# The beginning of a hybrid GLA/MLA/GQA trunk kernel: squares of the inputs first, two modulation blocks in a row, weight pieces and heads' weights later

## What is computed

```python
for l in range(DEPTH):                                   # DEPTH = 2
    shift, scale, gate = split(silu(c) @ w_mod[l] + b_mod[l], 3)          # latent tokens
    shift_c, scale_c, gate_c = split(silu(c_ctx) @ w_mod[l] + b_mod[l], 3)  # context tokens
    h  = rms_norm(x, norm_w[l]) * (1 + scale) + shift
    hc = rms_norm(ctx, norm_w[l]) * (1 + scale_c) + shift_c
    u, uc = split_cols(h @ w_in[l]), split_cols(hc @ w_in[l])
    y = concat(gla(u, uc), mla(u, uc), gqa(u, uc))       # three attention branches
    x = x + gate * (y @ w_out[l])                        # and ctx likewise in layer 0
return rms_norm(x, final_norm_w)
```

## Time and profile before

| | us |
|---|---|
| median of 3 runs | 1052.84 |
| lowest and highest | 1051.81, 1054.33 |
| the profiled execution | 1052.06 |
| its span in the profile | 1050.1 |
| TensorE busy in it | 963.9 (92%) |
| VectorE, ScalarE, GpSimd busy | 510.0, 421.4, 136.5 |
| mean granted TensorE clock | 0.971 of full |

### The profile page before, as it was taken

How to read it: one execution, slowest core, us unless ns; L and a number is a source line. 1 busy time by engine, 2 the same in 40 slices (tenths; PEclk the granted TensorE clock), 3 DMA queues, 4 the chain that set the end, 5 groups by cost and what they waited for, 6 DMA issues and landing times.

```text
span 1050.1 us, 12554 instructions
## 1 busy us (share of the span) xinstructions
PE 963.9 (92%) x4563; PEld 668.7 (64%) x4563; DVE 510.0 (49%) x872; ACT 421.4 (40%) x753; POOL 136.5 (13%) x158
## 2 busy tenths in 40 slices
PE   2789999999899999899899889899997999999896
PEld 2468889888465455455478677689774545445475
DVE  2535534532864444556452563543548444555443
ACT  4424433322113554656831432533321244555902
POOL 3000000001250001000640200000013300100720
PEclk9899999999889999999999899899999899999998
DMA  9802220311300232022053211130513000022022
GB/s 331 282 16 65 62 75 6 101 41 47 114 1 1 94 130 97 1 81 81 1 172 73 81 30 51 43 98 1 137 40 126 1 0 1 1 81 80 1 100 81
DMA packets 67867, 74.12 MB, mean 71 GB/s; under 512 B 6148, under 2 KB 47456, under 8 KB 67680
## 3 DMA queue, kind: packets, MB, share of 16 engines
q1 hardware_dynamic: 61392, 60.17, 18.2%
q0 software_dynamic: 4016, 12.77, 3.4%
q10 hardware_dynamic: 2400, 0.38, 0.2%
HBM read 69.11 MB, written 4.19 MB: 70 GB/s over the span
## 4 chain that ended last, share of the span: by engine, by line
PE 81%; DVE 7%; ACT 4%; issue 3%; DMA 2%; POOL 1%; ACTq 1%; DVEq 0%; POOLq 0%
PE pv L1692 10%; PE bank L1483 9%; PE bank L1484 9%; PE bank L1485 8%; PE bank L1743 6%; PE bank L1653 3%; PE bank L1774 3%; PE bank L1776 3%; PE bank L1775 3%; PE bank L1620 2%; PE bank L1600 2%; DMA W<-in_w_in 2%; PE bank L1669 2%; PE bank L1521 2%; PE bank L1523 2%
## 5 line engine op out<-in xcount | busy, mean ns | idle before, releaser
L1483 PE MATMUL bank<-hA_parts,W_parts 128*128 128x512 f32 (+1 forms) x496 | 181.7, 366 | 11.7 <-DVE h_low_parts L1016 9.1
L1484 PE MATMUL bank<-hA_parts,W_parts 128*128 128x512 f32 (+1 forms) x496 | 175.2, 353 | 0.0
L894 ACT ACTIVATE hA<-bank 128x512 f32<-128x512 f32 (+1 forms) x168 | 92.5, 561 | 82.1 <-PE bank L1743 56.1
L1290 DVE TENSOR_REDUCE mxp<-bank 128x1 f32<-128x384 f32 x192 | 96.4, 550 | 47.4 <-PE bank L1653 47.1
L1483 PEld LDWEIGHTS bank<-hA_parts,W_parts 128*128 128x128 f32 x496 | 95.7, 193 | 30.8 <-issue 14.0
L1485 PE MATMUL bank<-h_low_parts,W_parts 128*128 128x512 f32 (+1 forms) x310 | 109.9, 354 | 0.0
L1484 PEld LDWEIGHTS bank<-hA_parts,W_parts 128*128 128x128 f32 x496 | 95.6, 193 | 13.7 <-issue 2.2
L1692 PE MATMUL pv<-hA,vg 128*128 128x512 f32 (+1 forms) x168 | 83.1, 576 | 6.8 <-ACT hA L894 6.4
L1692 PE MATMUL pv<-hA,XA 128*128 128x512 f32 (+1 forms) x168 | 81.0, 563 | 2.4 <-ACT hA L894 2.3
L1023 DVE TENSOR_TENSOR W_parts<-W,W_parts 128x1024 fp32r<-128x1024 f32 x44 | 53.5, 1221 | 32.9 <-ACT W_parts L631 32.8
L1308 DVE SCALAR_TENSOR_TENSOR hA<-pv,hA 64x512 f32<-64x512 f32 (+1 forms) x36 | 21.6, 599 | 90.8 <-ACT hA L837 90.6
(11 more groups left out here) (254 smaller groups left out, 1836.6 us busy)
## 6 DMA issues: line engine op xcount, KB each, us to landing
W<-in_w_in SPq DMA_DIRECT2D x39, 512.0 KB, 4.0
W<-in_w_mod SPq DMA_DIRECT2D x8, 2048.0 KB, 8.0
W<-in_w_out SPq DMA_DIRECT2D x4, 2048.0 KB, 7.8
gqk<-in_w_mod SPq DMA_DIRECT2D x2, 1536.0 KB, 10.5
cqkv<-in_w_mod SPq DMA_DIRECT2D x2, 1536.0 KB, 14.7
XA<-in_x SPq DMA_DIRECT2D x4, 512.0 KB, 7.7
XA<-in_x POOLq DMA_DIRECT2D x4, 512.0 KB, 6.6
x_between_layers<-XA POOLq DMA_DIRECT2D x4, 512.0 KB, 2.9
```

The costliest lines, as they stand in the source:

```text
L894: act.activation(prob[slot % 4][:, 0:nq], ps("sc", l, h, q0, kt)[:, 0:nq], ACT.Exp, scale=MLA_SCALE if h < MLA_H else GQA_SCALE)\
L1290: dve.tensor_reduce(mxp[:, t, half:half + 1], ps("mx", l, h, q0, t, half)[:, 0:384], AX, ALU.max).then_inc(*up("part_max", l, h, q0, t, half))
L1483: pe.matmul(p[:, 0:c[1]], high[:, k, :], h_hi[:, k, toks], start=(k == 0), stop=False)
L1484: pe.matmul(p[:, 0:c[1]], low[:, k, :], h_hi[:, k, toks], start=False, stop=False)
```

## The change

ScalarE's queue starts with the identity. ScalarE no longer waits for the transposed vector tile before the squares: one table is loaded, the six tiles are squared, and only then the condition is computed, as exp(min(c,0) - ln(1 + exp(-|c|))) times c, with functions of that one table. TensorE transposes the vector tile behind the fourth input tile; VectorE copies it there and does its two steps of the condition between the copies of the last two tiles.

Modulation block 1 gets a ring bank and a row buffer of its own, so blocks 0 and 1 are multiplied in a row and then turned. ScalarE and VectorE take both blocks' rows and columns first, then units 0 and 1, slice 0, unit 2 and the other slices. TensorE multiplies block 2 after step k=0 and block 3 after k=1 of the product loop (before: after k=0 and k=2), and turns them after k=1 and k=2 (before: k=1 and k=3). GpSimd's `layer_weights(0)` moves behind the rearrangement of the narrow unit and a wait for block 3's products.

```diff
@@ -344,3 +344,7 @@
-            return pv_banks[0] if l == 0 and b < 4 else ps("mod", l, b)
+            return pv_banks[0] if l == 0 and b in (0, 2, 3) else ps("mod", l, b)
+        def modrow_of(l, b):
+            return cumA[:, 0:512] if (l, b) == (0, 1) else modrow
@@ -451,3 +455,2 @@
-            layer_weights(0)
             for l in range(DEPTH):
@@ -458,2 +461,5 @@
                 pool.memset(w_units[:, 0, 0, :, 32:64], 0.0).then_inc(*up("swap_kr", l))
+                if l == 0:
+                    pool.wait_ge(*at("filled", "mod", 0, 3))
+                    layer_weights(0)
                 pool.wait_ge(*at("wu_in", l))
@@ -551,2 +557,4 @@
         def _(act):
+            act.dma_start(con[:, C_ID:C_ID + P], a["consts"][:, C_ID:C_ID + P]).then_inc(*dma("ident_in"))
             def rows(r, n, src):
@@ -564,3 +572,2 @@
                     act.dma_start(vec[r:r + 2, half * 64:half * 64 + 64], a[name]).then_inc(*dma("vec_in"))
-            act.dma_start(con[:, C_ID:C_ID + P], a["consts"][:, C_ID:C_ID + P]).then_inc(*dma("ident_in"))
@@ -569,5 +576,2 @@
                 act.dma_start(w_units[:, 0, 0, :, o:o + n], src[:, :, c:c + n]).then_inc(*dma("w_small", 0))
-            act.wait_ge(*at("vec_turned"))
-            act.activation(ct[:, 0, :], vt[:, 0:16], ACT.Tanh, scale=0.5).then_inc(*up("cond_tanh"))
             act.preload_act_table_set("natural_log_exp_and_others")
@@ -578,5 +582,5 @@
-                    if (l, b) != (0, 0):
+                    if (l, b) not in ((0, 0), (0, 1)):
                         act.wait_ge(*at("filled", "modT", *((l, b - 1) if b else (l - 1, 3))))
-                    act.activation(modrow, mod_bank(l, b)[:], ACT.Copy).then_inc(*up("modrow", l, b))
+                    act.activation(modrow_of(l, b), mod_bank(l, b)[:], ACT.Copy).then_inc(*up("modrow", l, b))
                     let_go(("mod", l, b), "modrow", l, b)
@@ -655,2 +659,10 @@
                             turned_copy(t - 1)
+                    act.wait_ge(*at("vec_turned"))
+                    act.activation(ct[:, 0, :], vt[:, 0:16], ACT.Abs).then_inc(*up("cond_abs"))
+                    act.wait_ge(*at("cond_abs"))
+                    act.activation(ct[:, 0, :], ct[:, 0, :], ACT.Exp, scale=-1.0).then_inc(*up("cond_exp"))
+                    act.wait_ge(*at("cond_exp"))
+                    act.activation(ct[:, 0, :], ct[:, 0, :], ACT.Ln, bias=ones[:, 0:1]).then_inc(*up("cond_ln"))
+                    act.wait_ge(*at("cond_logsig"))
+                    act.activation(ct[:, 1, :], ct[:, 1, :], ACT.Exp).then_inc(*up("cond_sig"))
                     turned_copy(TILES - 1)
@@ -658,11 +670,13 @@
                     act.wait_ge(*at("xr_dve", TILES - 1, 1))
+                    mod_rows(0, 0)
+                    mod_rows(0, 1)
                     unit_high(0)
-                    for half in range(2):
-                        for b in range(2):
-                            mod_rows(0, 2 * half + b)
-                            if not half and b:
-                                unit_high(1)
-                                unit_high(2)
-                        for k in range(4):
-                            modulate(4 * half + k)
+                    unit_high(1)
+                    modulate(0)
+                    unit_high(2)
+                    for k in range(1, KD):
+                        if k == 4:
+                            mod_rows(0, 2)
+                            mod_rows(0, 3)
+                        modulate(k)
                     unit_high(3)
@@ -939,15 +953,19 @@
         def _(dve):
-            dve.wait_ge(*at("filled", "vec"))
-            dve.tensor_copy(vt[:], ps("vec")[:, 0:V_ROWS]).then_inc(*up("vec_turned"))
-            let_go(("vec",), "vec_turned")
-            dve.wait_ge(*at("vec_turned"))
-            dve.tensor_scalar(vth[:], vt[:], 0.5, None, ALU.mult).then_inc(*up("vec_half"))
-            dve.wait_ge(*at("cond_tanh"))
-            dve.wait_ge(*at("vec_half"))
-            dve.wait_ge(*at("pool_init", "end"))
-            dve.scalar_tensor_tensor(out=sc[:, :, 0:2].rearrange("p k s -> p s k"),
-                                     in0=ct[:, 0, :].rearrange("p (s k) -> p s k", s=2), scalar=1.0,
-                                     in1=vth[:, 0:16].rearrange("p (s k) -> p s k", s=2),
-                                     op0=ALU.add, op1=ALU.mult).then_inc(*up("cond_silu"))
+            def condition(part):
+                if part == 0:
+                    dve.wait_ge(*at("filled", "vec"))
+                    dve.tensor_copy(vt[:], ps("vec")[:, 0:V_ROWS]).then_inc(*up("vec_turned"))
+                    let_go(("vec",), "vec_turned")
+                if part == 1:
+                    dve.wait_ge(*at("cond_ln"))
+                    dve.scalar_tensor_tensor(out=ct[:, 1, :], in0=vt[:, 0:16], scalar=0.0, in1=ct[:, 0, :],
+                                             op0=ALU.min, op1=ALU.subtract).then_inc(*up("cond_logsig"))
+                    dve.wait_ge(*at("cond_sig"))
+                    dve.wait_ge(*at("pool_init", "end"))
+                    dve.tensor_tensor(sc[:, :, 0:2].rearrange("p k s -> p s k"),
+                                      vt[:, 0:16].rearrange("p (s k) -> p s k", s=2),
+                                      ct[:, 1, :].rearrange("p (s k) -> p s k", s=2), ALU.mult)\
+                        .then_inc(*up("cond_silu"))
+                    dve.tensor_scalar(vth[:], vt[:], 0.5, None, ALU.mult).then_inc(*up("vec_half"))
@@ -1007,2 +1025,5 @@
                     turned_copy(t - 1)
+                if t == TILES - 2:
+                    condition(0)
+            condition(1)
             turned_copy(TILES - 1)
@@ -1026,11 +1047,13 @@
                 if l == 0:
+                    mod_cols(0, 0)
+                    mod_cols(0, 1)
                     unit_low(0)
-                    for half in range(2):
-                        for b in range(2):
-                            mod_cols(0, 2 * half + b)
-                        if not half:
-                            unit_low(1)
-                            unit_low(2)
-                        for k in range(4):
-                            split_hidden(4 * half + k)
+                    unit_low(1)
+                    split_hidden(0)
+                    unit_low(2)
+                    for k in range(1, KD):
+                        if k == 4:
+                            mod_cols(0, 2)
+                            mod_cols(0, 3)
+                        split_hidden(k)
                     unit_low(3)
@@ -1422,7 +1445,2 @@
-            pe.wait_ge(*at("vec_in"))
-            pe.wait_ge(*at("ident_in"))
-            p = open_("vec")
-            close(pe.transpose(p[:, 0:V_ROWS], vec, ident[0:V_ROWS, 0:V_ROWS]), "vec")
             def mod(l, b):
@@ -1430,5 +1448,5 @@
                 if l == 0 and b < 4:
-                    p, w = mod_bank(l, b), early[b % 2]
-                    if b:
-                        pe.wait_ge(*at("modrow", l, b - 1))
+                    p, w = open_("mod", l, b) if b == 1 else mod_bank(l, b), early[b % 2]
+                    if b >= 2:
+                        pe.wait_ge(*at("modrow", l, b - 1 if b > 2 else 0))
                     pe.wait_ge(*at(f"w_early{b % 2}", b))
@@ -1458,3 +1476,3 @@
                     for f in range(4):
-                        mm = pe.transpose(q[:, P * f:P * f + P], modrow[:, P * f:P * f + P], ident)
+                        mm = pe.transpose(q[:, P * f:P * f + P], modrow_of(l, b)[:, P * f:P * f + P], ident)
                     close(mm, "modT", l, b)
@@ -1466,2 +1484,3 @@
+            pe.wait_ge(*at("ident_in"))
             for t in range(TILES):
@@ -1474,2 +1493,6 @@
                     close(mm, "xr", t, half)
+                if t == TILES - 3:
+                    pe.wait_ge(*at("vec_in"))
+                    p = open_("vec")
+                    close(pe.transpose(p[:, 0:V_ROWS], vec, ident[0:V_ROWS, 0:V_ROWS]), "vec")
@@ -1490,2 +1513,3 @@
                 mod(0, b)
+            for b in range(2):
                 mod_turn(0, b)
@@ -1497,6 +1521,9 @@
                         close(mm, "F", 0, item, c)
-                if k in (0, 2):
-                    mod(0, 2 + k // 2)
-                if k in (1, 3):
-                    mod_turn(0, 2 + k // 2)
+                if k == 0:
+                    mod(0, 2)
+                if k == 1:
+                    mod_turn(0, 2)
+                    mod(0, 3)
+                if k == 2:
+                    mod_turn(0, 3)
```

## The result

The changed kernel takes 1040.28 us in the median (1039.05 to 1041.91, 4 runs) beside 1052.32 for the kernel before (1050.71 to 1054.33, 4 runs): a ratio of 0.9885 with a 95% interval of 0.987 to 0.9901. 1041.6 had been forecast.

What follows compares the result with a forecast made beforehand. TensorE, 81% of the chain of waits, was taken to bound the kernel through early idles and half clock behind them. 9.5 + 1.7 = 11.2 us off 1052.06 gave 1040.9, median 1041.6; own range 1039 to 1044, overall 1036.5 to 1047.5.

Steps and rivals of the forecast that it cites:

- The sum: Whole run: 9.5 us at the product loop's fifth step plus 1.7 from the second half-clock stretch, 11.2 us gained.
- step 4: Heads' weights issued later: block 1's weights land near 25, the three pieces at 28.4 to 29.1; moved transfers cost nothing.
- Step 1: Squares first: first square at 9.94 instead of 15.86, 5.92 us earlier; three small condition steps add 0.75.
- Step 2: Modulation blocks 0 and 1 back to back, 1.9 us each; columns at 29.95, 6.4 us gained there.
- Step 3: Weight pieces behind the rows: first product of hidden values at 34.1 against 40.35, 6.25 us earlier.
- rival (a): Freed DMA time does not reach the other queues, landings stay: gain 8.1 us, 1044.7; chance 0.17.
- Step 5: Blocks 2 and 3 earlier in product loop: idle 0.65 instead of 3.70, fifth step 54.2 against 63.72, 9.5 us.
- The clock term: Second half-clock stretch, behind the fifth step's idle, goes with that idle: 1.7 us, half of its 3.40.
- Rival (c): Something else holds the fifth step at the second stall; only the start's 6.25 us remain: 1046.6; chance 0.07.
- (b): The first half-clock stretch at the first products shrinks too, giving back 1.9 us: 1039.7; chance 0.08.
- (d): Low clock persists over the first steps; if twice as long, 1.9 to 3.4 us lost: 1043.5 to 1045; chance 0.05.
- (e): TensorE's clock stays at half from first product through all eight steps: slower, 1065; chance 0.02.

Runs made afterwards that it cites:

- squares only: Kernel before with only the identity first, squares first and the condition behind them in one table's functions; 1052.56 us, ratio 0.9998.
- one-bank run: Changed kernel with blocks 0 and 1 sharing one bank and row buffer again, each turned before the next is multiplied; 1042.49 us, ratio 0.9902.

## Why the prediction was right

**The sum.** 11.2 was forecast up to the eighth step; the traces show 11.76 there, and the medians differ by 12.0 and, with the changed kernel once more, by 11.6. The forecast of 1041.6 is 1.3 above the measured median, inside its own range of 1039 to 1044.

That it came so close is in part luck. The first product came 1.4 us before the forecast, the fifth step only 0.7: the low stretch took half of it back. And two misses covered each other. With the start a microsecond early, block 1 began at 24.79 and the rounding of piece 1 near 28.2; step 4 had their weights land near 25 and at 28.4 to 29.1, which would have been late for both. They landed at 23.6 and 27.7.

**Step 1** had the right place; block 0 started 1.0 before the forecast. The three small steps behind the copies took 0.69 (0.75 was said), no table load appeared among them, and the vector transpose was hidden. What I missed is that ScalarE's own issues got shorter: its queue's last two transfers took 1.10 to issue, and the first square came at 9.05 rather than 9.94. Counting it in the sum would have given 1040.7. The same two took 1.08 with the identity first and the weights early (squares only: 1.06), 1.36 with the identity behind and the weights late, 2.17 with both as before. By these rows, of one execution each, either edit shortens them, and the identity's new place does so by itself.

**Step 2** held: from block 0's start it is 1.74 us to block 1's (1.9 was said) and 5.8 to the columns at 28.85 (5.9 was said). The second bank is worth the 1.4 us at the first product that the one-bank run shows.

**Step 3** held in the main: from the columns to the first product 3.9 us, and 4.15 was said. Its claim that the pieces belong behind the rows is not borne out for piece 0: the run with it ahead shows 0.8 us less idle, and with one bank the new order brought nothing at the first product. For pieces 1 and 2 no run puts them ahead. The start's gain comes from the squares, the late weights and the second bank.

**Step 4** is what the experiments confirm most clearly. Landings near 25 and 28.4 to 29.1 were forecast, 23.6 and 27.7 came. With the weights early again block 1 waits 4.13 us for them, which is rival (a)'s state; its 1044.7 compares with 1045.8. Rival (a) falls as a description of the change. What came forward, 5.5 us, was more than the 4.0 to 4.7 by bytes and by time; why, no run shows. The transfers moved behind block 3 were hidden: wa is read at 85.5, and GpSimd had rearranged wuq by 62.2.

```profile
53.07 1.16 POOL L450 DMA_DIRECT2D wuq<-in_mla_w_uq  x1
57.29 1.65 POOL L453 DMA_DIRECT2D wukv<-in_mla_w_ukv  x2 [3.06 <-issue]
```

Of the rule of the Trainium skill (SBUF — State Buffer, "SBUF: two separate sides"), which I had put at up to 1.2 us per transfer, these rows beside a busy VectorE show at most 0.3: 1.16 for an issue that took 0.88 at 47.47, and 1.65 for two. The issue of 1.16 is the only one of them within which one of VectorE's casts lay whole (53.27 to 53.83). The first four issues, from 46.35 to 49.19, met no VectorE operation at all, since VectorE stood idle until 49.83. The rule changed nothing, as said.

**Step 5** and the second stall: idle 0.65 forecast, 0.56 measured; 3.71 without the new places. The fifth step came 10.2 us earlier (9.5 was said). The clock term was 1.7; the mark moved 1.54 more than the fifth step. Rival (c) falls by the runs with and without the places.

**The clock.** The first low stretch was kept in the sum at its old cost. In the first profile it cost more (the first step took 5.7, not 5.18), in the second less. Rivals (b) and (d) are thus two sides of what varies from one execution to the next, about 1 us; (e) did not come near. What lies between 11.76 and the 13.2 of the span is such a difference too: the stretch at 266.9 was 3.2 us longer than its counterpart at 256.5, which at half clock is about the 1.4 found. That one profile of each explains it is an argument, not a test.

## What to carry to other kernels

When an engine waits for work and the next thing in line is a transfer that lands at about the same time, removing either wait alone can show next to nothing (0 and 2 us in the medians here, 6 together); so ask of each wait what is late next before dropping an edit that measured as nothing. Loads that are read much later should not share the DMA engines with the first ones, even on a queue of their own: 1.39 MB moved out of the way brought the needed ones forward by over 5 us. Put a small dependent chain at the latest place in a pipeline loop that still leaves its whole latency covered by products, since cutting an idle of 3.7 us to 0.55 brought 4.0 us at the mark, with the clock that no longer fell behind it.

## What the runs showed of the hardware

An idle of TensorE costs more than its length in two ways: the stretch behind it (3.4 us at 0.50 before the change), and the work released by the wait itself, as block 1's ten matmuls took 2.77 and 2.10 behind waits of 4.13 and 2.89 for a DMA, 2.47 where TensorE had stood still for 4.00 us shortly before them, and 1.46 to 1.48 elsewhere. Where the low stretch begins beside the same idle of 4.51 varied by 1.4 us between two executions of the same kernel (31.4 and 32.8), it lasted 6.65 us in the one and 3.4 in the other, and the mark moved by 1.0 us with it. And the time in which ScalarE issues a transfer depended on the other transfers: the same two transfers took between 1.06 and 2.17, with what stood before them on the queue and beside them on GpSimd's (one execution each).
